# The last 64 inner columns of a gated FFN: gate and up in one product, high and low parts in one k tile

## The chip, the cores and the metric

The kernel runs on one core of one Trainium2 chip. The metric is the device time of one execution in microseconds. The time before the change is the median of three runs, 2739.53 us (2738.53 to 2741.1). Every time below of a single instruction comes from one profiled execution, which took 2738.45 us; its span, from the first to the last instruction, is 2736.7 us.

## The reference, cut to what matters

Three layers work on 512 tokens of width 1024. Each has an FFN, a mixer and a second FFN, so six FFNs in all. The first four have an inner width of 2816, which is 22 tiles of 128. The two of the last block have an inner width of 2752, which is 21.5 tiles:

```python
D_FF_2 = 2752
def swiglu_2(h, w_gate, w_up, w_down):
    return (jax.nn.silu(h @ w_gate) * (h @ w_up)) @ w_down

x = x + 0.5 * swiglu_2(rms_norm_2(x, ffn1_norm), ffn1_w_gate, ffn1_w_up, ffn1_w_down)
...
x = x + 0.5 * swiglu_2(rms_norm_2(x, ffn2_norm), ffn2_w_gate, ffn2_w_up, ffn2_w_down)
```

## The kernel before

**Layout.** Activations are kept feature-major: a tile holds 128 features in its partitions and 512 tokens in its columns. X is 8 such tiles, the inner activation of an FFN is 22 of them. A product takes a 128x128 block of weights as the stationary operand and a tile of activations as the moving one, and adds into one of 8 PSUM banks.

**Precision.** Each factor is split in a high part (float32r) and a low part (the rest), and a product is three matmuls: low weights by high activations, high by low, high by high. That is the helper `mm3` (lines 418, 419, 420). Where the profile names L418, L419 and L420 it means these three. Xh and Xl are the parts of the FFN's input, Hh and Hl those of its inner activation, wh and wl those of a chunk of weights.

**Weights.** `weight_stream` lists all weights once, as chunks of up to 128 x 1024 numbers, in the order in which TensorE takes them. Each chunk goes through a ring of three buffers (`N_RAW`): SP's `fetch` loads it to `raw` (lines 2039 to 2048) once the chunk three before it has been split; ScalarE's `high` writes wh (L889) and VectorE's `low` writes wl (L1265), both only after TensorE has finished with the chunk three before. Each of these two engines calls `use`, which splits up to two chunks ahead (`AHEAD`) of what TensorE is due to take; so the splits stand between the engine's other work, in an order fixed by the program.

**An FFN** is a stage `s`; s = 7 and s = 9 have the inner width 2752. In `ffn(s)` TensorE goes over blocks j of 256 inner columns: gate for two tiles, then up for the same two, each from two chunks of 4 k tiles by 256 columns. Block j uses banks 0 to 3 if j is even, 4 to 7 if odd; in each half the gates stand in the lower two and the ups in the upper two. For each inner tile VectorE and ScalarE then do in turn: gate times the norm factor r (VectorE, L1274), silu (ScalarE, L957), up times r, times silu (VectorE, L1274), copy to Hh (ScalarE, L920), subtract to Hl (VectorE, L1274). The down product (`residual`) makes output tiles in groups of two, two, two, one and one (`DOWN`), each over all 22 k tiles; at k tile k it waits for Hh and Hl of tile k. In s = 9 the eighth output tile is made in two halves of 256 tokens (`last_tile`).

**The odd width.** `tile_width` gives the last two inner tiles, 20 and 21, 96 columns each, 192 together. So the last block (j = 10) makes two gate and two up products that give 96 partitions each, from chunks 4 x 192 = 768 wide, and the last two k tiles of every down product contract over 96 rows (`tail` in `proj` and `last_tile`). The rows of w_down for them are laid out by a separate DMA with 96 partitions (`parts` in `chunks`), and where they share a chunk with full tiles (output tiles 6 and 7) `high` and `low` take two instructions for that chunk.

Of the kernel before, what the change touches and what calls it, by code (L numbers as in the profile page):

```python
# [13 lines left out]
D = 1024  # L14
# [81 lines left out]

def chunks(w, k0, k1, n0, n1, per=None):

    n = n1 - n0
    per = per or min(4, CAP // n)
    got = []
    for k in range(k0, k1, per * 128):
        top = min(k1, k + per * 128)
        full, rest = divmod(top - k, 128)
        nk = full + (rest > 0)
# [15 lines left out]
def chunks_ffn(wg, wu, wd, first=False):  # L123

    f, got = wg.shape[1], []
    for n0 in range(0, f, 256):
        n1 = min(f, n0 + 256)
# [4 lines left out]
        got += chunks(wg, 0, D, n0, n1, 4) + chunks(wu, 0, D, n0, n1, 4)  # L132
    return got + chunks_down(wd, f)
# [41 lines left out]
def build(nc, a, out):  # L175
    ctx = ExitStack()
    with ctx:
# [55 lines left out]
        def parts_of(n, bufs):  # L233
            parts, width, _ = stream[n]
            return [bufs[n % N_RAW][0:rows, k0 * width:(k0 + nk) * width] for rows, k0, nk, _ in parts]
# [160 lines left out]
        def tensor_program(e, w):  # L396
# [27 lines left out]
            def proj(outs, widths, kt, hi, lo, ready, hooks, tail=128):  # L424
# [4 lines left out]
                while k < kt:  # L429
                    n, h, l, nk = chunk()  # L430
                    for kk in range(nk):
                        p, last = tail if k + kk >= kt - 2 else 128, k + kk == kt - 1
                        ready(k + kk)
                        for m, wd in enumerate(widths):
                            sl = slice(sum(widths[0:m]), sum(widths[0:m + 1]))
                            names = [outs[m][1]] if last else []
                            if kk == nk - 1 and m == len(widths) - 1:
                                names.append(("used", n))
                            mm3(into[m][0:wd, :], h[0:p, kk, sl], l[0:p, kk, sl], hi[0:p, k + kk, :],
                                lo[0:p, k + kk, :], k + kk == 0, last, *names)  # L440
# [35 lines left out]
            def residual(s, tile_bank, hi, lo, kt, ready, tail=128):  # L476
                for t0, t1, _ in DOWN if s < 9 else DOWN[0:-1]:
                    proj([(tile_bank(t), ("down", s, t)) for t in range(t0, t1)], [128] * (t1 - t0), kt, hi, lo, ready,
                         None, tail)

            def last_tile(s, hi, lo, kt, tail):
# [20 lines left out]
                for part, (q0, q1) in enumerate(HALVES):  # L502
                    name = ("down", s, 7, part)
                    bank = take(LAST[part][0], name)
                    for k in range(kt):
                        if k == len(rows):
# [3 lines left out]
                        p, last = tail if k >= kt - 2 else 128, k == kt - 1  # L510
                        mm3(bank[:, q0:q1], h[0:p, kk, :], l[0:p, kk, :], hi[0:p, k, q0:q1], lo[0:p, k, q0:q1], k == 0, last,
                            *([name] if last else []))
# [7 lines left out]
            def ffn(s):  # L520
# [3 lines left out]
                for j, n0 in enumerate(range(0, f, 256)):  # L524
                    widths = [tile_width(s, 2 * j + m) for m in range(2)]
                    for side, b in (("gate", 0), ("up", 2)):
                        outs = [(4 * (j % 2) + b + m, (side, s, 2 * j + m)) for m in range(len(widths))]
                        proj(outs, widths, KT, Xh, Xl, x_ready(s) if j == 0 else lambda k: None, hooks)
# [5 lines left out]
                residual(s, lambda t: (4 + t) % 8, *H, nt, ready, tile_width(s, nt - 1))  # L534
                if s == 9:
                    last_tile(s, *H, nt, tile_width(s, nt - 1))
# [338 lines left out]
        def scalar_program(e, w):  # L875
# [3 lines left out]
            def high():  # L879
# [8 lines left out]
                for hi, src in zip(parts_of(n, wh), parts_of(n, raw)):  # L888
                    e.activation(hi, src, ACT.Copy).then_inc(whi.up(("w", n)), 1)  # L889
# [52 lines left out]
            def ffn(s):  # L942
                f, gain = FFN[s]
                nt = -(-f // 128)
                for j in range(-(-nt // 2)):
# [5 lines left out]
                    else:  # L951
                        use(4)
# [298 lines left out]
        def vector_program(e, w):  # L1251
# [3 lines left out]
            def low():  # L1255
# [8 lines left out]
                for lo, hi, src in zip(parts_of(n, wl), parts_of(n, wh), parts_of(n, raw)):  # L1264
                    e.tensor_tensor(lo, src, hi.bitcast(F), ALU.subtract).then_inc(wlo.up(("w", n)), 1)  # L1265
# [923 lines left out]
```

## Time and profile before

| | |
|---|---|
| median of 3 runs | 2739.53 us |
| the profiled execution | 2738.45 us |
| its span | 2736.7 us |
| TensorE matmuls | 12604, busy 99% of the span |
| VectorE busy | 49% |
| ScalarE busy | 33% |
| DMA | 252.3 MB, mean 92 GB/s |
| mean granted TensorE clock | 0.998 of full |
| last gate and up block of s = 7 | starts at 2038.15 us |
| down product of s = 7 | 2060.40 us to about 2180 us |
| last gate and up block of s = 9 | starts at 2581.42 us |
| down product of s = 9 | 2603.67 us to about 2726 us |

In the profile a matmul's duration (about 0.39 us) is longer than the time from its start to the start of the next (0.22 to 0.23 us), since matmuls are pipelined. So sums of durations say nothing of the time; the distance of starts does. A line of the timeline gives start, duration, engine, line, operation, output <- inputs, shape and count. In a matmul's row `128*96` is the stationary operand, 128 rows by 96 columns, and `128x512` the moving one. Some matmul records are missing from the trace, so counts are taken from the program.

### The profile page before, as it was taken

What the parts mean: (1) busy time and instruction counts of PE and PEld (TensorE: products, weight loads), DVE (VectorE), ACT (ScalarE), POOL (GpSimd) and SP (SyncE); (2) the same over time, 40 slices, a digit from 0 to 9 for tenths busy, and PEclk for the clock granted to TensorE, in tenths of its full rate; (3) what the DMA queues carried; (4) which work ended last, traced back from release to release, by engine and by line L of the source; (5) the groups of instructions that cost most, each with busy time, mean ns of one, the idle gap of its engine ahead of it and who ended that gap; (6) DMA issues with size and microseconds to landing.
All of it is one profiled execution on the core that took longest, in us unless ns stands there. A gap on an engine that the chain in (4) does not pass through costs nothing.

```text
span 2736.7 us, 31462 instructions
## 1 busy us (share of the span) xinstructions
PE 2711.6 (99%) x12604; PEld 2257.7 (82%) x12604; DVE 1341.3 (49%) x1918; ACT 900.5 (33%) x1287; POOL 135.2 (5%) x133
## 2 busy tenths in 40 slices
PE   9999999999999999999999999999999999999998
PEld 7888878888888888888888888888888898888787
DVE  5444358764443444443655444344443478644433
ACT  4232226542222323222223232223222337432221
POOL 0000004400000000000000000000000034000000
PEclk9999999999999999999999999999999999999999
DMA  4332332023333333323333323333332321233322
GB/s 158 100 94 96 95 92 72 24 93 102 99 96 95 98 98 99 98 88 101 100 99 94 93 93 98 100 96 93 101 93 91 97 78 47 62 104 98 91 91 75
DMA packets 283121, 252.30 MB, mean 92 GB/s; under 512 B 8288, under 2 KB 280800, under 8 KB 282976
## 3 DMA queue, kind: packets, MB, share of 16 engines
q1 hardware_dynamic: 282976, 250.29, 29.8%
q8 instruction: 101, 1.65, 0.2%
q14 instruction: 44, 0.36, 0.0%
HBM read 248.16 MB, written 2.10 MB: 91 GB/s over the span
## 4 chain that ended last, share of the span: by engine, by line
PE 97%; DVE 1%; ACT 1%; issue 0%; DMA 0%; POOLq 0%; POOL 0%; DVEq 0%; SPq 0%; ACTq 0%
PE bank L418 32%; PE bank L420 32%; PE bank L419 32%; PE bank L550 1%; PE bank L460 0%; PE bank L608 0%; PE bank L609 0%; DVE a_KT L1277 0%; ACT Xh L920 0%; DVE Xl L1274 0%; DVE ft L1274 0%; DMA X<-in_xT 0%; DVE fin L1277 0%; DVE wl L1265 0%; ACT a_RB L920 0%
## 5 line engine op out<-in xcount | busy, mean ns | idle before, releaser
L1265 DVE TENSOR_TENSOR wl<-raw,wh 128x1024 fp32r<-128x1024 f32 (+3 forms) x492 | 572.6, 1177 | 924.1 <-ACT wh L889 923.5
L418 PE MATMUL bank<-Xh,wl 128*128 128x512 f32 (+1 forms) x2544 | 994.0, 391 | 7.5 <-DVE wl L1265 6.6
L420 PE MATMUL bank<-Xh,wh 128*128 128x512 f32 (+1 forms) x2544 | 991.3, 390 | 0.0
L419 PE MATMUL bank<-Xl,wh 128*128 128x512 f32 (+1 forms) x2544 | 990.9, 390 | 0.0
L889 ACT ACTIVATE wh<-raw 128x1024 fp32r<-128x1024 f32 (+3 forms) x492 | 491.7, 1014 | 952.8 <-PE bank L420 947.8
L418 PEld LDWEIGHTS bank<-Xh,wl 128*128 128x128 f32 (+1 forms) x2544 | 475.8, 187 | 111.4 <-ACT wh L889 6.1
L420 PEld LDWEIGHTS bank<-Xh,wh 128*128 128x128 f32 (+1 forms) x2544 | 475.7, 187 | 102.8
L419 PEld LDWEIGHTS bank<-Xl,wh 128*128 128x128 f32 (+1 forms) x2544 | 476.0, 187 | 100.8
L418 PE MATMUL bank<-Hh,wl 128*128 128x512 f32 (+3 forms) x1078 | 415.1, 385 | 0.0
L419 PE MATMUL bank<-Hl,wh 128*128 128x512 f32 (+3 forms) x1078 | 414.9, 385 | 0.0
L420 PE MATMUL bank<-Hh,wh 128*128 128x512 f32 (+3 forms) x1078 | 414.7, 385 | 0.0
L1274 DVE TENSOR_TENSOR ft<-bank,rb 128x512 f32<-128x512 f32 (+1 forms) x264 | 181.5, 688 | 171.5 <-PE bank L420 112.2
L418 PEld LDWEIGHTS bank<-Hh,wl 128*128 128x128 f32 (+1 forms) x1078 | 202.5, 188 | 40.5
L419 PEld LDWEIGHTS bank<-Hl,wh 128*128 128x128 f32 (+1 forms) x1078 | 202.6, 188 | 40.5
L420 PEld LDWEIGHTS bank<-Hh,wh 128*128 128x128 f32 (+1 forms) x1078 | 202.5, 188 | 40.4
L920 ACT ACTIVATE Hh<-ft 128x512 fp32r<-128x512 f32 (+1 forms) x132 | 83.5, 632 | 269.0 <-DVE ft L1274 269.0
L957 ACT ACTIVATE ft<-ft 128x512 f32<-128x512 f32 (+1 forms) x132 | 83.5, 632 | 208.6 <-DVE ft L1274 208.6
L1274 DVE TENSOR_TENSOR Hl<-ft,Hh 128x512 fp32r<-128x512 f32 (+1 forms) x132 | 91.3, 692 | 92.2 <-ACT Hh L920 92.2
L1274 DVE TENSOR_TENSOR ft<-ft,ft 128x512 f32<-128x512 f32 (+1 forms) x132 | 91.4, 692 | 4.5
L917 ACT ACTIVATE Xh<-X,par 128x512 fp32r<-128x512 f32 x64 | 46.1, 723 | 128.0 <-DVE X L1277 108.4
L1895 POOL TENSOR_TENSOR r<-small,half 128x4 f32<-128x4 f32 (+1 forms) x11 | 10.5, 957 | 1376.1 <-DVE small L1283 1376.1
L1277 DVE SCALAR_TENSOR_TENSOR Xl<-X,par,Xh 128x512 fp32r<-128x512 f32 x64 | 47.8, 750 | 38.3 <-ACT Xh L917 38.0
(289 smaller groups left out, 1568.3 us busy)
## 6 DMA issues: line engine op xcount, KB each, us to landing
raw<-in_ffn_w_up SPq DMA_DIRECT2D x128, 512.0 KB, 3.9
raw<-in_ffn_w_gate SPq DMA_DIRECT2D x127, 512.0 KB, 3.6
raw<-in_ffn_w_down SPq DMA_DIRECT2D x114, 512.0 KB, 3.5
raw<-in_c_w_in SPq DMA_DIRECT2D x24, 512.0 KB, 3.6
raw<-in_w_in SPq DMA_DIRECT2D x10, 512.0 KB, 3.7
raw<-in_ffn_w_down SPq DMA_DIRECT2D x16, 256.0 KB, 2.7
raw<-in_a_w_in SPq DMA_DIRECT2D x8, 512.0 KB, 3.8
raw<-in_a_w_out SPq DMA_DIRECT2D x8, 512.0 KB, 3.4
```

What stands on the lines that cost most here:

```text
L418: e.matmul(o, ll, rh, start=start, stop=False)
L419: e.matmul(o, lh, rl, start=False, stop=False)
L420: i = e.matmul(o, lh, rh, start=False, stop=stop)
L550: e.transpose(bank[0:rows, t * 128:(t + 1) * 128], src, ident).then_inc(mm.up(name), 1)
L889: e.activation(hi, src, ACT.Copy).then_inc(whi.up(("w", n)), 1)
L917: e.activation(Xh[:, t, :], X[:, t, :], ACT.Copy, scale=col(gain, t)).then_inc(act.up(("xh", s, t)), 1)
L920: e.activation(dst, src, ACT.Copy, scale=scale).then_inc(act.up(*names), 1)
L957: e.activation(B[0:wd, :], A[0:wd, :], ACT.Silu).then_inc(act.up(("silu", s, ht)), 1)
L1265: e.tensor_tensor(lo, src, hi.bitcast(F), ALU.subtract).then_inc(wlo.up(("w", n)), 1)
L1274: e.tensor_tensor(dst, a, b, op).then_inc(dve.up(*names), 1)
L1277: e.scalar_tensor_tensor(dst, a, scalar, b, op0, op1).then_inc(dve.up(*names), 1)
L1895: e.tensor_tensor(dst, a, b, op).then_inc(pool.up(*names), 1)
```

## The change

The inner columns are cut otherwise: tiles 0 to 20 have 128 columns, and tile 21 has 64. Tile 20 gets a gate product and an up product of its own, each from one chunk of 8 k tiles by 128 columns. For tile 21 one chunk holds the 64 gate columns and the 64 up columns beside each other, and one product makes both: gate in partitions 0 to 63 of bank 1, up in partitions 64 to 127. VectorE reads up, the norm factor for it, and writes the low part of the result, in partitions 64 to 127; gate, silu and the high part stay in partitions 0 to 63. So k tile 21 of `Hh` holds the high part above and the low part below. The chunk of w_down for this k tile has its 64 rows twice, once for each half. The down product then takes two matmuls for this tile (`mm2`: low weights by both, high weights by both) and contracts over 128 rows. In the ring of chunks, the last block has three chunks and not four.

```diff
+def rows_of(w, k0, k1, n0, n1):
+    return w[k0:k1, n0:n1].rearrange("(k p) n -> p k n", p=min(128, k1 - k0))
 # chunks()
+        cut = k + full * 128
+        moves = [(0, (0, n), 0, rows_of(w, k, cut, n0, n1))] if full else []
         if rest:
-            full -= 1
-        parts = []
-        if full:
-            parts.append((128, 0, full, w[k:k + full * 128, n0:n1].rearrange("(k p) n -> p k n", p=128)))
-        if rest:
-            parts.append((64 + rest // 2, full, 2, w[k + full * 128:top, n0:n1].rearrange("(k p) n -> p k n", k=2)))
-        got.append((parts, n, nk))
+            moves += [(row, (0, n), full, rows_of(w, cut, top, n0, n1)) for row in (0, 64)]
+        got.append((moves, n, full + (rest > 0)))
 # chunks_ffn()
+    if f % 256:
+        n0, n1 = f - 192, f - 64
+        got += chunks(wg, 0, D, n0, n1, 8) + chunks(wu, 0, D, n0, n1, 8)
+        got.append(([(0, (0, 64), 0, rows_of(wg, 0, D, n1, f)), (0, (64, 128), 0, rows_of(wu, 0, D, n1, f))], 128, KT))
 # tile_width()
-            f = FFN[s][0]
-            return 64 + f % 128 // 2 if f % 128 and ht >= f // 128 - 1 else 128
+            return min(128, FFN[s][0] - 128 * ht)
 # tensor_program
+            def mm2(o, h, l, both, *names):
+                e.matmul(o, l, both, start=False, stop=False)
+                i = e.matmul(o, h, both, start=False, stop=True)
 # proj()
-                        p, last = tail if k + kk >= kt - 2 else 128, k + kk == kt - 1
+                        last = k + kk == kt - 1
...
+                            if half and last:
+                                mm2(into[m][0:wd, :], h[:, kk, sl], l[:, kk, sl], hi[:, k + kk, :], *names)
 # ffn() on TensorE
+                if f % 256:
+                    for b, name in ((0, ("gate", s, nt - 2)), (2, ("up", s, nt - 2)), (1, ("gate", s, nt - 1))):
+                        proj([(b, name)], [128], KT, Xh, Xl, lambda k: None, hooks)
+                    mm.also(("up", s, nt - 1))
 # ScalarE high(), VectorE low(): one instruction for every chunk
-                for hi, src in zip(parts_of(n, wh), parts_of(n, raw)):
-                    e.activation(hi, src, ACT.Copy).then_inc(whi.up(("w", n)), 1)
+                e.activation(part_of(n, wh), part_of(n, raw), ACT.Copy).then_inc(whi.up(("w", n)), 1)
 # ffn() on ScalarE and VectorE, last block
-                        use(4)
+                        use(4 if 2 * j < f // 128 - 1 or f % 256 == 0 else 3)
 # ffn() on VectorE
+                        low = H[1][:, ht, :]
...
+                            tt(A, gate, r, ALU.mult, ("g", s, ht))
+                            up, r, low = banks[1][64:128, :], rb[s % 2][64:128, :], H[0][64:128, ht, :]
...
-                        tt(H[1][0:wd, ht, :], A, H[0][0:wd, ht, :].bitcast(F), ALU.subtract, ("hl", s, ht))
+                        tt(low, A, H[0][0:wd, ht, :].bitcast(F), ALU.subtract, ("hl", s, ht))
 # fetch() on SP
-                for (_, _, _, src), dst in zip(parts, parts_of(n, raw)):
-                    e.dma_start(dst.rearrange("p (k n) -> p k n", n=width), src).then_inc(raw_in[r].sem, 16)
+                for row, (c0, c1), k0, src in moves:
+                    dst = raw[r][row:row + src.shape[0], 0:nk * width].rearrange("p (k n) -> p k n", n=width)
+                    e.dma_start(dst[:, k0:k0 + src.shape[1], c0:c1], src).then_inc(raw_in[r].sem, 16)
```

## Rows read from the trace of the kernel before

**Rows 1.** The page's first part: busy time of each engine and instructions.
```profile
PE 2711.6 (99%) x12604; PEld 2257.7 (82%) x12604; DVE 1341.3 (49%) x1918; ACT 900.5 (33%) x1287; POOL 135.2 (5%) x133
```

**Rows 2.** The page's fourth part: the chain that ended last, by engine.
```profile
PE 97%; DVE 1%; ACT 1%; issue 0%; DMA 0%; POOLq 0%; POOL 0%; DVEq 0%; SPq 0%; ACTq 0%
```

**Rows 3.** Groups by shape: operation, shapes, count, busy us, mean ns, idle before, releaser.
```profile
L418 PE MATMUL bank<-Xh,wl 128*128 128x512 f32 x2472 | 965.7, 391 | 7.5 <-DVE wl L1265 6.6 <-ACT g_P L973 0.8
```

**Rows 4.** Timeline, TensorE: eight k tiles into one bank, in the convolution mixer.
```profile
1310.45 0.39 PE L418 MATMUL bank<-Xh,wl 128*128 128x512 f32 x1
...
1315.89 0.39 PE L418 MATMUL bank<-Xh,wl 128*128 128x512 f32 x1
```

**Rows 5.** Timeline, TensorE, s = 7: last gate and up block, first k tiles of down.
```profile
2038.15 0.39 PE L418 MATMUL bank<-Xh,wl 128*96 128x512 f32 x1
...
2060.40 0.40 PE L418 MATMUL bank<-Hh,wl 128*128 128x512 f32 x1
...
2087.61 0.40 PE L418 MATMUL bank<-Hh,wl 96*128 96x512 f32 x1
...
2090.36 0.40 PE L418 MATMUL bank<-Hh,wl 128*128 128x512 f32 x1
```

**Rows 6.** Timeline, TensorE, s = 9: start and end of the last block.
```profile
2581.42 0.39 PE L418 MATMUL bank<-Xh,wl 128*96 128x512 f32 x1
...
2603.67 0.40 PE L418 MATMUL bank<-Hh,wl 128*128 128x512 f32 x1
```

**Rows 7.** Timeline, TensorE: k tiles 20 and 21 of single and half output tiles.
```profile
2163.93 0.40 PE L418 MATMUL bank<-Hh,wl 96*128 96x512 f32 x1
...
2165.32 0.40 PE L418 MATMUL bank<-Hh,wl 128*128 128x512 f32 x1
...
2715.79 0.28 PE L418 MATMUL bank<-Hh,wl 96*128 96x256 f32 x1
...
2716.51 0.28 PE L418 MATMUL bank<-Hh,wl 128*128 128x256 f32 x1
```

**Rows 8.** Timeline, VectorE, s = 7: around the start of the last block and its end.
```profile
2033.84 0.96 DVE L1265 TENSOR_TENSOR wl<-raw,wh 128x768 fp32r<-128x768 f32 x1 [4.48 <-ACT wh L889]
...
2040.39 0.69 DVE L1274 TENSOR_TENSOR ft<-bank,rb 128x512 f32<-128x512 f32 x1
...
2043.96 0.69 DVE L1274 TENSOR_TENSOR Hl<-ft,Hh 128x512 fp32r<-128x512 f32 x1 [0.70 <-ACT Hh L920]
2044.69 1.83 DVE L1265 TENSOR_TENSOR wl<-raw,wh 128x768 fp32r<-128x768 f32 x2
...
2066.18 0.69 DVE L1274 TENSOR_TENSOR Hl<-ft,Hh 96x512 fp32r<-96x512 f32 x1 [0.70 <-ACT Hh L920]
2067.13 2.36 DVE L1265 TENSOR_TENSOR wl<-raw,wh 128x1024 fp32r<-128x1024 f32 x2 [0.26 <-ACT wh L889]
```

**Rows 9.** Timeline, ScalarE, the same stretch; one split of a full chunk.
```profile
2043.83 1.57 ACT L889 ACTIVATE wh<-raw 128x768 fp32r<-128x768 f32 x2
2049.53 1.06 ACT L889 ACTIVATE wh<-raw 128x1024 fp32r<-128x1024 f32 x1 [4.14 <-PE bank L420]
```

**Rows 10.** Groups by shape, VectorE on 64 partitions.
```profile
L1274 DVE TENSOR_TENSOR Xl<-bank,Xh 64x512 fp32r<-64x512 f32 x16 | 11.0, 687 | 12.2 <-ACT Xh L920 11.9
```

**Rows 11.** DMA issues: count, KB each, median us from issue to landing.
```profile
raw<-in_c_w_in SPq DMA_DIRECT2D x24, 512.0 KB, 3.6
raw<-in_ffn_w_gate SPq DMA_DIRECT2D x4, 384.0 KB, 3.3
raw<-in_ffn_w_down SPq DMA_DIRECT2D x6, 192.0 KB, 2.4
```

**Rows 12.** Timeline, SP's queue: the issue of the third chunk of the last block.
```profile
2025.58 4.23 SPq L2046 DMA_DIRECT2D raw<-in_ffn_w_up  x2
```

**Rows 13.** Stretches of 2 us in the first mixer: busy times, then PEclk.
```profile
468.00:470.00 2.00, 0.17 (x2) 0.00 (x0) 1.97 (x9) 1.18 (x4) 1.43 (x2) 1.00 0.14 18
470.00:472.00 2.00, 1.88 (x12) 1.68 (x13) 1.97 (x10) 0.64 (x4) 2.00 (x7) 0.85 0.71 244
472.00:474.00 2.00, 2.00 (x10) 1.91 (x9) 1.96 (x9) 0.45 (x2) 2.00 (x3) 0.50 0.00 0
474.00:476.00 2.00, 2.00 (x13) 1.87 (x12) 0.95 (x6) 1.30 (x6) 1.39 (x4) 0.80 0.00 0
```

More of the change, by code:

```diff
@@ L125, in chunks_ffn @@
     f, got = wg.shape[1], []
-    for n0 in range(0, f, 256):
-        n1 = min(f, n0 + 256)
+    for n0 in range(0, f // 256 * 256, 256):
+        n1 = n0 + 256
         if first and n0 == 0:
@@ L231, in build, with part_of @@
         stream = weight_stream(a)
-        def parts_of(n, bufs):
-            parts, width, _ = stream[n]
-            return [bufs[n % N_RAW][0:rows, k0 * width:(k0 + nk) * width] for rows, k0, nk, _ in parts]
+        def part_of(n, bufs):
+            _, width, nk = stream[n]
+            return bufs[n % N_RAW][:, 0:nk * width]
         def views(n):
@@ L422, in mm3, with proj @@
                     i.then_inc(mm.up(*names), 1)
-            def proj(outs, widths, kt, hi, lo, ready, hooks, tail=128):
+            def mm2(o, h, l, both, *names):
+                e.matmul(o, l, both, start=False, stop=False)
+                i = e.matmul(o, h, both, start=False, stop=True)
+                if names:
+                    i.then_inc(mm.up(*names), 1)
+            def proj(outs, widths, kt, hi, lo, ready, hooks, half=False):
                 into = [take(*o) for o in outs]
@@ L438, in proj @@
                                 names.append(("used", n))
[L439 to L440 removed]
+                            if half and last:
+                                mm2(into[m][0:wd, :], h[:, kk, sl], l[:, kk, sl], hi[:, k + kk, :], *names)
+                            else:
+                                mm3(into[m][0:wd, :], h[:, kk, sl], l[:, kk, sl], hi[:, k + kk, :], lo[:, k + kk, :],
+                                    k + kk == 0, last, *names)
                     k += nk
@@ L474, in stats, with residual, last_tile @@
                 return sums, spread
-            def residual(s, tile_bank, hi, lo, kt, ready, tail=128):
+            def residual(s, tile_bank, hi, lo, kt, ready, half=False):
                 for t0, t1, _ in DOWN if s < 9 else DOWN[0:-1]:
                     proj([(tile_bank(t), ("down", s, t)) for t in range(t0, t1)], [128] * (t1 - t0), kt, hi, lo, ready,
-                         None, tail)
-            def last_tile(s, hi, lo, kt, tail):
+                         None, half)
+            def last_tile(s, hi, lo, kt):
                 rows = []
@@ L509, in last_tile @@
                         h, l, kk = rows[k]
-                        p, last = tail if k >= kt - 2 else 128, k == kt - 1
-                        mm3(bank[:, q0:q1], h[0:p, kk, :], l[0:p, kk, :], hi[0:p, k, q0:q1], lo[0:p, k, q0:q1], k == 0, last,
-                            *([name] if last else []))
+                        if k == kt - 1:
+                            mm2(bank[:, q0:q1], h[:, kk, :], l[:, kk, :], hi[:, k, q0:q1], name)
+                        else:
+                            mm3(bank[:, q0:q1], h[:, kk, :], l[:, kk, :], hi[:, k, q0:q1], lo[:, k, q0:q1], k == 0, False)
                         if part == 1 and k == 6:
@@ L1356, in ffn @@
                     else:
-                        use(4)
+                        use(4 if 2 * j < f // 128 - 1 or f % 256 == 0 else 3)
                     for ht in range(2 * j, min(2 * j + 2, nt)):
```

25 lines of the change are left out of this document (13 added, 12 removed).

## Prediction

> **What bounds the kernel now.** I read the busy times first, then the chain that ended last, then the groups by shape, and only then the timeline of the two stages that the change touches. TensorE is busy 99% of the span [rows 1] and holds 97% of the chain [rows 2]. The largest of its groups, 2472 matmuls, stood idle for 7.5 us in all, and 6.6 of those were waits for VectorE's weights [rows 3]. So the time is TensorE's, and an instruction taken from it gives back its pitch (the distance from one matmul's start to the next), as long as the weights and the inner activation still come in time. The price is the pitch and not the duration: eight k tiles of three matmuls into one bank take 5.44 us, 0.2267 us for each [rows 4], while each lasts 0.39 us.
>
> **The gate and up side.** Before, the last block of s = 7 is 2 gates and 2 ups over 8 k tiles, 2 x 2 x 8 x 3 = 96 matmuls with 96 columns of weights. They take 2060.40 - 2038.15 = 22.25 us, 0.2318 us each [rows 5]; s = 9 takes the same 22.25 us [rows 6]. After, it is three products of 8 k tiles, 72 matmuls with 128 columns. A bank that takes all eight k tiles in a row has a row of its own, at 0.2267 us [rows 4], so 72 of them are 16.32 us. Saved: 5.93 us in each FFN, 11.86 us. Of these 24 x 0.2267 = 5.44 us per FFN are the matmuls that go, and 0.49 us is the slower pitch of the narrow ones.
>
> **A rule of the notes.** The narrow block's pitch is 0.2318 us, the full one's 0.2267 [rows 4, 5]. The Trainium skill ("TensorE: Matmul & The Clock Gate", Back-to-back issue gap) gives an isolated matmul of 512 columns 518 cycles of the fast clock, whatever the number of weight columns; that would be an estimated 0.216 us for either. The trace differs in both. By that page the sum would be 64 matmuls' worth of 0.216, some 13.8 us.
>
> **The down side.** Before, the last two k tiles are six matmuls per output tile with 96 rows. After, they are five with 128 rows. For a pair of output tiles the twelve took 2090.36 - 2087.61 = 2.75 us [rows 5], and ten take 10 x 0.2267 = 2.27 us: 0.48 us saved, three pairs in each FFN, 1.44 us. For a single output tile six took 1.39 us [rows 7], and five take 1.13 us: 0.26 us saved, twice in s = 7 and once in s = 9. The halves of the last tile of s = 9 took 0.72 us for six, 0.12 us each [rows 7]; one less in each half saves 0.24 us. Down side: 1.44 + 0.52 = 1.96 us in s = 7 and 1.44 + 0.26 + 0.24 = 1.94 us in s = 9, 3.90 us.
>
> **The sum** is 11.86 + 3.90 = 15.8 us. The profiled execution (2738.45 us, span 2736.7) would come to 2722.7 us with a span of 2720.9; the median of the runs shown lies 1.1 us higher, and from it the forecast is 2739.53 - 15.8 = 2723.8 us.
>
> **What has to stay hidden: the splits.** Call T = 2038.15 the start of the last block. The third chunk is needed at T + 10.88 (two chunks of 24 matmuls). VectorE ends the two inner tiles of the block before at 2044.65, T + 6.5 [rows 8]. ScalarE starts the high part of the third chunk at 2043.83, T + 5.7, and a full chunk takes it 1.06 us [rows 9]; VectorE's low part follows at T + 6.75 and lasts 1.2 us (two took 2.36 [rows 8]), so it is ready at T + 8.0. The slack is 2.9 us. Before, the third chunk was ready at about T + 7.5 and needed at T + 11.1, 3.6 us. Two earlier splits grow from 768 to 1024 columns, 0.96 to 1.2 us on VectorE; the first steps of the tile behind them (gate, silu) shift by some 0.3 us, and then the chain waits for its up product, which ends near T anyway.
>
> The block now ends at T + 16.3 = E. In front of it VectorE's order is: low part of the third chunk, of the first down chunk (T + 8.0 to 9.2), of the second, which waits until TensorE is done with the up chunk at T + 10.88 (high, then low, to T + 13.2); then tile 20, then tile 21. Queued behind that wait is tile 20, whose gate was ready at T + 5.44; nobody needs it early. A tile's chain lasts from 2040.39 to 2044.65, 4.3 us [rows 8]: tile 20 is done at T + 17.5 = E + 1.2, tile 21 at E + 5.4. Before, both were done at 2066.87, which is 6.5 us after the block's end [rows 5, 8]. Next are the splits of the third and fourth down chunk. They follow by 0.3 to 1.5 us, the first ready at E + 7.0; TensorE needs it at E + 10.88, 3.9 us of slack against 3.0 before (ready at 2067.13 + 1.18 = 2068.3, needed at 2060.40 + 10.88 = 2071.3 [rows 5, 8]). The down product itself meets k tile 20 only 120 matmuls later, at E + 27.2, and tile 21 six later. All waits inside the change are covered, and the one behind the block is covered better. The fewer split instructions on ScalarE and VectorE (one instead of two for the last chunks of output tiles 6 and 7, one chunk less) are off the path and cost or give nothing.
>
> **Other parts.** The partition shift: two VectorE operations on tile 21 (up times r, and the low part) read and write at different partitions. No row of before shows a shifted operation. The nearest is 64 partitions from PSUM at 0.687 us [rows 10], and the full width costs 0.69 too [rows 8]; a shift could cost nothing, or, as an upper bound, one more pass of the same length, 0.69 us each. I take 0; at the bound 1.4 us more go into a slack of 3.9. A gain is excluded, since the chain isn't on the path. Banks: the last block takes banks 0, 2 and 1, read long before; down's first pair takes banks 4 and 5, whose last reading (the gate of tile 19, 2040.39 to 2041.08 [rows 8]) lies 13 us before E. Loads: 64 rows of w_down go twice, by three DMAs instead of one or two. A tail chunk of 192 KB lands in 2.4 us [rows 11]; three issues on SP, each of the size of one now, bound it at three times that, 7.2 us, and below at 2.4. It is the last chunk of six, fetched three chunks ahead of its use (at least two full chunks of TensorE, 10.9 us), so either end costs nothing. The `use(3)` keeps both splitting engines in step with three chunks.
>
> **The load of the combined chunk.** It is two DMAs of 256 KB, in pieces of 64 columns, 256 bytes; the chunk of before it had pieces of 768 bytes and landed in 3.3 us [rows 11]. The convolution's chunks are 512 KB in 1024 pieces of 512 bytes and land in 3.6 us [rows 11]. The new one has 2048 pieces: 3.6 us if bytes count, 7.2 us if pieces do. It is issued once the chunk three before it is split, at 2025.58 [rows 12], and ScalarE wants it at 2043.83 [rows 9]: 18.2 us. Both ends fit, I take zero. The Trainium skill ("DMA: Bandwidth & Descriptors", Specifications) says that a transfer wants at least 512 bytes per piece for line rate and that a smaller one is a read-modify-write. No row of before shows pieces of 256 bytes; what that rule could do here is the second rival.
>
> **The rivals.**
> *A, VectorE is late behind the shifted operations.* If the two of them cost so much that the third down chunk comes late, each microsecond above 3.9 us is TensorE's. Against it: [rows 10]. A stall has a price of its own: after a stop of 2 us in the first mixer [rows 13] the granted clock was 0.50 for some 3.4 us (0.85, 0.50 and 0.80 over three stretches of 2 us), from 1.00, that is 1.2 GHz instead of 2.4, which gives back 1.7 us less work. With a stall of 2 us in each FFN, and 1.7 us behind each, this case gives 2723.8 + 7.4 = 2731.2 us.
> *B, the combined chunk lands too late (the other side).* Its small pieces may be so slow that ScalarE waits for the load. TensorE begins to lose when landing takes more than 18.2 + 2.9 = 21.1 us, about three times the upper bound of 7.2. A stall then costs its length plus 1.7 us of clock [rows 13], in two FFNs; the whole gain of 15.8 us is lost at a stall of 6.2 us each, landing in 27.3 us, and 0.2% more than that at 30. With pieces four times as dear as in the convolution's chunk (28.8 us) the stall is 7.7 us, 2 x 9.4 = 18.8 us against 15.8: 2742.5 us, about as before, and above 30 us slower. For it: nothing in the rows but their silence.
> *C, only the count helps.* The slow pitch of 0.2318 belongs to the place and not to the 96 columns: then 72 x 0.2318 = 16.7 us and 10 and 5 matmuls at 0.229 on the down side, a loss of 0.37 and about 0.08 us per FFN: 2724.7 us. Against it: the 120 matmuls right behind the block, with the same engines beside them, take 27.21 us, 0.2268 each [rows 5].
> *D, the change doesn't do what it says:* the three products would not follow each other without a gap, because each is a new bank and a new chunk every 24 matmuls. Against it: the convolution does the same for 24 products with no gap in the one that is shown [rows 4]. I give it no time of its own; a few tenths at each of three starts lie inside the range.
>
> **How the numbers follow.** About 0.2% (5.5 us) is what a measurement of this kernel can tell from no change, so faster means below 2734.1 us. Forecast 0.84, C 0.06, A 0.06 (2731, still faster, but its longer stalls reach the middle), B 0.04, half of it at no change and half slower. Range: below, the sum against the lowest of the runs before gives 2722.7, and one more microsecond is the spread of medians, so 2721; above, C at 2724.7, the highest of the runs before less the sum (2725.3) and stalls of A's kind up to 1.5 us per FFN give 2729. Faster 0.94, within 0.2% 0.04, slower 0.02.
>
> **What would show it.** In the trace after: 72 matmuls of 128 x 128 between the last block's start and the first down matmul, 16.3 us, in both FFNs; no matmul with 96 rows or columns on Xh or Hh with 512 tokens; k tiles 20 and 21 of a pair in 2.27 us; the two FFNs 7.9 us shorter each and all else alike; idle before L418 still about 7.5 us. Rival A would show as idle time of TensorE some 11 us after the down product starts, released by wl; B as a wait of ScalarE's split for a DMA from w_gate or w_up; C as a pitch above 0.227 in the last block. The prediction is wrong if a new stretch with a granted clock of 0.5 appears in s = 7 or s = 9.

## The result and the profile after

The changed kernel takes 2723.57 us (median of four runs, 2723.0 to 2724.64) against 2740.32 us (four runs, 2738.53 to 2742.66): a ratio of 0.9940, 95% interval 0.9928 to 0.9952, 16.75 us less. A second set of five runs gave 2723.57 us again, ratio 0.9939 (0.9926 to 0.9953). The forecast was 2723.8 us.

The profiled execution took 2723.5 us, its span is 2721.7 us; the span of before was 2736.7, so it shows 15.0 us. The page's first and fourth part after:

```profile
PE 2696.8 (99%) x12539; PEld 2252.2 (83%) x12539; DVE 1341.3 (49%) x1912; ACT 899.7 (33%) x1281; POOL 135.1 (5%) x133
PE 97%; DVE 1%; ACT 1%; issue 0%; DMA 0%; POOLq 0%; POOL 0%; DVEq 0%; SPq 0%; ACTq 0%
```

There are 65 matmuls fewer, as the edit says: 24 in each last block, 8 in the down product of s = 7, 7 and two halves in that of s = 9. The busy shares, which answer to [rows 1], and the chain [rows 2] have not moved, so this page alone would not tell where the 15 us went. The largest group, by shape as in [rows 3], comes with the line numbers of the new file (L423, L424 and L425 are `mm3`, L431 and L432 `mm2`, L1282 the low split, L1292 VectorE's tensor_tensor, L907 the high split, L2070 the load):

```profile
L423 PE MATMUL bank<-Xh,wl 128*128 128x512 f32 x2520 | 984.8, 391 | 7.5 <-DVE wl L1282 6.6 <-ACT g_P L991 0.8
```

Idle before it is 7.5 us as before. No new wait has come, and from 480 us to 2714 us, which takes in both FFNs, the mean granted clock is 1.00: the stretch at 0.5 that would have made the prediction wrong is in neither. The timeline of TensorE in s = 7 answers to [rows 5], with one line of s = 9 and two of its last halves:

```profile
2039.33 0.39 PE L423 MATMUL bank<-Xh,wl 128*128 128x512 f32 x1
...
2055.65 0.39 PE L423 MATMUL bank<-Hh,wl 128*128 128x512 f32 x1
...
2084.21 0.39 PE L431 MATMUL bank<-Hh,wl 128*128 128x512 f32 x1
2084.44 0.39 PE L432 MATMUL bank<-Hh,wh 128*128 128x512 f32 x1
2084.67 0.39 PE L431 MATMUL bank<-Hh,wl 128*128 128x512 f32 x1
2084.89 0.39 PE L432 MATMUL bank<-Hh,wh 128*128 128x512 f32 x1
2085.12 0.39 PE L423 MATMUL bank<-Hh,wl 128*128 128x512 f32 x1
...
2590.89 0.39 PE L423 MATMUL bank<-Hh,wl 128*128 128x512 f32 x1
```

The last block lasts 2055.65 - 2039.33 = 16.32 us, to the hundredth what the sum had. A pair of output tiles lasts 2085.12 - 2055.65 = 29.47 us, where [rows 5] had 2090.36 - 2060.40 = 29.96. The splits behind the block, which answer to [rows 8]:

```profile
2046.10 2.36 DVE L1282 TENSOR_TENSOR wl<-raw,wh 128x1024 fp32r<-128x1024 f32 x2 [0.26 <-ACT wh L907]
...
2058.19 0.69 DVE L1292 TENSOR_TENSOR ft<-bank,rb 64x512 f32<-64x512 f32 x1 [0.70 <-ACT ft L975]
2058.92 0.68 DVE L1292 TENSOR_TENSOR ft<-ft,ft 64x512 f32<-64x512 f32 x1
2060.30 0.69 DVE L1292 TENSOR_TENSOR Hh<-ft,Hh 64x512 fp32r<-64x512 f32 x1 [0.70 <-ACT Hh L938]
2061.25 2.42 DVE L1282 TENSOR_TENSOR wl<-raw,wh 128x1024 fp32r<-128x1024 f32 x2 [0.27 <-ACT wh L907]
```

The first and the third of the 64-partition lines are the shifted operations: 0.69 us each, no dearer than an unshifted one. With T the start of the last block and E its end, as in the prediction, the third chunk of the block is ready at 2046.10 + 1.18 = 2047.28, T + 7.95; tile 21 ends at 2060.99, E + 5.3; the third down chunk is ready at 2062.46, E + 6.8. The combined chunk's two loads were issued at 2026.77 and 2027.19, and each took a few microseconds:

```profile
2026.77 0.37 SPq L2070 DMA_DIRECT2D raw<-in_ffn_w_gate  x1
2027.19 0.57 SPq L2070 DMA_DIRECT2D raw<-in_ffn_w_up  x1
...
raw<-in_ffn_w_up SPq DMA_DIRECT2D x2, 256.0 KB, 4.7
```

**Stage by stage.** I take the distance between the small matmuls that sum squares, of which one group of eight stands near the start of each stage, and the first down matmul within an FFN; the last row ends at the first of two matmuls of the final norm, just behind the last down product. In microseconds, from the profiled executions:

| stretch | before | after | difference |
|---|---|---|---|
| through s = 2 (the first mixer), from its statistics to those of s = 3 | 137.70 | 139.00 | +1.30 |
| s = 3 to s = 6, up to the statistics of s = 7 | 1256.83 | 1256.83 | 0.00 |
| s = 7 to its first down matmul | 230.38 | 224.44 | -5.94 |
| s = 7, from there to the statistics of s = 8 | 131.45 | 129.38 | -2.07 |
| s = 8 | 181.44 | 181.42 | -0.02 |
| s = 9 to its first down matmul | 230.38 | 224.44 | -5.94 |
| s = 9, from there to the last matmuls | 125.90 | 123.75 | -2.15 |

The two FFNs give back 8.01 and 8.09 us, 16.1 in all; the medians differ by 16.75, and their interval (13.2 to 19.7 us) holds both. Of the last row's 2.15 us, 2.03 lie before the last down matmul and 0.12 in the norm behind it. The 1.3 us that the profiled span doesn't show were lost in a stage that the change leaves alone: there the clock stayed at half for longer (below).

### The profile page after: what moved, and what is told of

Its sections match the earlier page's. It is cut to its first block, busy times and chain, and to the rows that moved or that the text cites. A ratio compares the mean times of both kernels' runs of the same rounds, so it can differ in the third digit from the quotient of the medians.

```text
span 2721.7 us, 31322 instructions
## 1 busy us (share of the span) xinstructions
PE 2696.8 (99%) x12539; PEld 2252.2 (83%) x12539; DVE 1341.3 (49%) x1912; ACT 899.7 (33%) x1281; POOL 135.1 (5%) x133
## 4 chain that ended last, share of the span: by engine, by line
PE 97%; DVE 1%; ACT 1%; issue 0%; DMA 0%; POOLq 0%; POOL 0%; DVEq 0%; SPq 0%; ACTq 0%
PE bank L423 32%; PE bank L425 32%; PE bank L424 32%; PE bank L569 1%; PE bank L475 0%; PE bank L627 0%; PE bank L628 0%; DVE a_KT L1295 0%; ACT Xh L938 0%; PE bank L431 0%; PE bank L432 0%; DVE Xl L1292 0%; DVE ft L1292 0%; DMA X<-in_xT 0%; DVE fin L1295 0%
## 5 line engine op out<-in xcount | busy, mean ns | idle before, releaser
L1282 DVE TENSOR_TENSOR wl<-raw,wh 128x1024 fp32r<-128x1024 f32 (+2 forms) x486 | 572.2, 1190 | 912.1 <-ACT wh L907 911.4
L423 PE MATMUL bank<-Xh,wl 128*128 128x512 f32 x2528 | 987.9, 391 | 7.5 <-DVE wl L1282 6.6
L425 PE MATMUL bank<-Xh,wh 128*128 128x512 f32 x2528 | 985.1, 390 | 0.0
L424 PE MATMUL bank<-Xl,wh 128*128 128x512 f32 x2528 | 985.1, 390 | 0.0
L907 ACT ACTIVATE wh<-raw 128x1024 fp32r<-128x1024 f32 (+2 forms) x486 | 490.9, 1024 | 940.9 <-PE bank L425 936.1
L423 PEld LDWEIGHTS bank<-Xh,wl 128*128 128x128 f32 x2528 | 474.8, 188 | 108.2 <-ACT wh L907 6.1
L425 PEld LDWEIGHTS bank<-Xh,wh 128*128 128x128 f32 x2528 | 474.8, 188 | 100.3
L424 PEld LDWEIGHTS bank<-Xl,wh 128*128 128x128 f32 x2528 | 474.9, 188 | 98.3
L423 PE MATMUL bank<-Hh,wl 128*128 128x512 f32 (+1 forms) x1061 | 408.5, 385 | 0.0
L425 PE MATMUL bank<-Hh,wh 128*128 128x512 f32 (+1 forms) x1061 | 408.3, 385 | 0.0
L424 PE MATMUL bank<-Hl,wh 128*128 128x512 f32 (+1 forms) x1061 | 408.3, 385 | 0.0
L1292 DVE TENSOR_TENSOR ft<-bank,rb 128x512 f32<-128x512 f32 x264 | 181.7, 688 | 167.9 <-PE bank L425 107.4
L424 PEld LDWEIGHTS bank<-Hl,wh 128*128 128x128 f32 x1061 | 199.3, 188 | 39.9
L425 PEld LDWEIGHTS bank<-Hh,wh 128*128 128x128 f32 x1061 | 199.3, 188 | 39.7
L423 PEld LDWEIGHTS bank<-Hh,wl 128*128 128x128 f32 x1061 | 199.3, 188 | 39.6
L1292 DVE TENSOR_TENSOR Hl<-ft,Hh 128x512 fp32r<-128x512 f32 x130 | 90.0, 692 | 90.8 <-ACT Hh L938 90.8
L1292 DVE TENSOR_TENSOR ft<-ft,ft 128x512 f32<-128x512 f32 x132 | 91.4, 692 | 4.5
```

The source lines that it names most:

```text
L423: e.matmul(o, ll, rh, start=start, stop=False)
L424: e.matmul(o, lh, rl, start=False, stop=False)
L425: i = e.matmul(o, lh, rh, start=False, stop=stop)
L907: e.activation(part_of(n, wh), part_of(n, raw), ACT.Copy).then_inc(whi.up(("w", n)), 1)
L1282: e.tensor_tensor(part_of(n, wl), part_of(n, raw), part_of(n, wh).bitcast(F), ALU.subtract).then_inc(wlo.up(("w", n)), 1)
L1292: e.tensor_tensor(dst, a, b, op).then_inc(dve.up(*names), 1)
```

## The experiments

The theory: the gain is the number of matmuls taken off TensorE times their pitch, plus the slower pitch of the 96-column ones, and all else has cover. Seven kernels were run for the terms and the covers, and four more for what these left open. Their edits are cut to what matters; `...` stands for lines left out.

**The changed kernel again**, beside the three below.

> The changed kernel once more, beside the three below. My theory (count of matmuls times pitch, and the narrow pitch and its switches gone) gives 16.0 us less than before: 8.0 in each of the two FFNs. If the step from 15.8 forecast to the measured medians were more than noise, the saving would come out near 16.8 again; if the missing 1.2 us of the profiled span is the clock after the stall in the first mixer, that stretch and no other shows it again or not, by chance.

It took 2723.57 us (2721.38 to 2724.7) beside a before of 2740.34 (22 runs). In its profile the FFNs are those of the table to 0.01 us. Only the first mixer differs again, 140.66 us. So the medians gave 16.8 us once more, where the stages of both profiles give 16.1: what the other 0.7 us are, no stage shows, and the intervals are wide enough for them to be noise.

**Only the gate and up side** (the same edit stands in `last_tile`).

```diff
-                                mm2(into[m][0:wd, :], h[:, kk, sl], l[:, kk, sl], hi[:, k + kk, :], *names)
+                                mm3(into[m][0:wd, :], h[0:64, kk, sl], l[0:64, kk, sl], hi[0:64, k + kk, :],
+                                    lo[0:64, k + kk, :], False, True, *names)
...
-                        low = H[1][:, ht, :]
+                        low = H[1][0:wd, ht, :]
...
-                            up, r, low = banks[1][64:128, :], rb[s % 2][64:128, :], H[0][64:128, ht, :]
+                            up, r = banks[1][64:128, :], rb[s % 2][64:128, :]
```

> Only the gate and up side of the change: three products of 24 in the last block, but the low part of tile 21 stands in its own buffer and k tile 21 of the down product is three matmuls over 64 rows, as three-part products are. By my sum 15 matmuls of 0.2267 us and two halves of 0.12 us come back, 3.6 us, and some 0.1 to 0.4 us more for switching between 128 and 64 rows: 3.6 to 4.0 us slower than the changed kernel, about 12.2 us faster than before. If the down side were worth nothing (hidden by something else), it would be as fast as the changed kernel.

It took 2732.20 us (ratio to before 0.9970, 0.9959 to 0.9982), 8.6 us slower than the changed kernel and not 3.6 to 4.0. The trace puts all of it in the two down products: 133.38 and 127.83 us, 4.00 and 4.08 more than in the changed kernel. That is even 1.9 us each more than before. Where it goes, from TensorE's timeline of s = 7 around the first visit to k tile 21:

```profile
2083.61 0.39 PE L425 MATMUL bank<-Hh,wh 128*128 128x512 f32 x1
2083.93 0.49 PE L423 MATMUL bank<-Hh,wl 64*128 64x512 f32 x1
2084.26 0.39 PE L424 MATMUL bank<-Hl,wh 64*128 64x512 f32 x1
...
2085.19 0.39 PE L425 MATMUL bank<-Hh,wh 64*128 64x512 f32 x1
2085.51 0.50 PE L423 MATMUL bank<-Hh,wl 128*128 128x512 f32 x1
2085.84 0.40 PE L424 MATMUL bank<-Hl,wh 128*128 128x512 f32 x1
```

The starts are 0.32 and 0.33 us apart where the stationary operand goes from 128 to 64 rows, and again where it goes back, instead of 0.23. So both sides of my theory were tried at once, count and switches; the run with a third matmul, below, parts them.

**Only the down side.** Tiles of 128 and 64 columns, gate and up in 96 matmuls as before, `mm2` in the down product. The edit is against the changed kernel; VectorE then reads up from partitions 0 to 63, and only the low part is shifted.

```diff
-        got += chunks(wg, 0, D, n0, n1, 8) + chunks(wu, 0, D, n0, n1, 8)
-        got.append(([(0, (0, 64), 0, rows_of(wg, 0, D, n1, f)), (0, (64, 128), 0, rows_of(wu, 0, D, n1, f))], 128, KT))
+        got += chunks(wg, 0, D, f - 192, f, 4) + chunks(wu, 0, D, f - 192, f, 4)
...
-                    for b, name in ((0, ("gate", s, nt - 2)), (2, ("up", s, nt - 2)), (1, ("gate", s, nt - 1))):
-                        proj([(b, name)], [128], KT, Xh, Xl, lambda k: None, hooks)
+                    for side, b in (("gate", 0), ("up", 2)):
+                        proj([(b, (side, s, nt - 2)), (b + 1, (side, s, nt - 1))], [128, 64], KT, Xh, Xl,
+                             lambda k: None, hooks)
```

> Only the down side: tiles of 128 and 64 columns, gate and up made by 96 matmuls (half of them 64 columns wide), the low part of tile 21 in the lower half of the high part's k tile, two matmuls for it. By my sum 3.9 us faster than before from the down side, and 0.1 to 0.5 us per FFN from the pitch of the block if the 64-column matmuls are slow (0.2318) or not: 4.2 to 5.2 us faster than before. If the whole gain were the block's, it would be no faster than before.

It took 2734.42 us (ratio 0.9981, 0.9972 to 0.9990), 5.9 us faster than before by the medians (the interval allows 2.7 to 7.7), 4.7 by the stages of its trace: 2.05 and 2.13 us in the down products (129.40 and 123.77, the changed kernel's own) and 0.28 in each block. By the stages it lies in the 4.2 to 5.2 us that were expected, by the medians above them. The down side's worth is as forecast, and it doesn't need the other side.

**The block with 128 weight columns**, in the kernel before.

```diff
+                            at = n % N_RAW
+                            if wd == 96:
+                                c = kk * 192 + 96 * m
+                                mm3(into[m][:, :], wh[at][:, c:c + 128], wl[at][:, c:c + 128], hi[:, k + kk, :],
+                                    lo[:, k + kk, :], k + kk == 0, last, *names)
+                                continue
```

> The kernel before, with 128 weight columns in each of the 96 matmuls of the last block instead of 96 (the 32 columns more are read from what stands behind in the buffer, and the 32 rows that they fill in the bank are read by nobody). My theory: the pitch goes from 0.2318 to 0.2267 us, the block from 22.25 to 21.76 us in both FFNs, 1.0 us in all. Rival C, the slow pitch belongs to the place: the block stays at 22.25 us and the time is that of before.

It took 2738.70 us (ratio 0.9996, 0.9987 to 1.0005). The block's first matmul and the first of the down product, in s = 7:

```profile
2036.99 0.39 PE L418 MATMUL bank<-Xh,wl 128*128 128x512 f32 x1
...
2059.24 0.39 PE L418 MATMUL bank<-Hh,wl 128*128 128x512 f32 x1
```

22.25 us, as with 96 columns. The narrow stationary operand is not what makes the block slow, or not alone. Nor is it the place (rival C): the changed kernel runs at 0.2267 us there. A full block of 128 columns makes its products in pairs too, like the narrow one, and has 0.227 us, so the order of the banks isn't it either. What is left is how the weights lie: 192 columns, 768 bytes, from one k tile to the next, and the second inner tile at byte 384. Two kernels take these apart.

**Another layout for the same 96 matmuls.**

```diff
+        if n1 - n0 == 192:
+            for w in (wg, wu):
+                for k in (0, 512):
+                    rows = w[k:k + 512, n0:n1].rearrange("(k p) n -> p k n", p=128)
+                    got.append(([(128, 0, 4, rows)], 256, 4))
+            continue
...
+                            if wd == 96:
+                                sl = slice(SECOND * m, SECOND * m + 96)
```

(In the kernel before, with the load as two DMAs, the second to column `SECOND`, 128 in the first kernel and 96 in the second.)

> The kernel before, with the same 96 matmuls of 96 columns in the last block, but the chunk laid out with 256 columns for each k tile and the two inner tiles at columns 0 and 128 of them (byte offsets 0 and 512), by two DMAs per chunk. Neither the number of weight columns nor the place in the program changes. The 128-column run at the old layout kept the slow block (22.25 us), so my term 'narrow columns are slow' has fallen. Theory now: the layout of the weights (a distance of 768 bytes between k tiles, an offset of 384) is slow; then this block takes 21.76 us in both FFNs, 1.0 us less in all. Rival: 96 columns or any layout but the changed kernel's own are slow, 22.25 us.

> The same, 256 columns for each k tile, but the second inner tile at column 96 (byte offset 384). If the distance of 768 bytes is what is slow, the block takes 21.76 us as above. If the offset of 384 bytes is, the second tile's half of the matmuls stay slow: between 21.9 and 22.25 us.

Both took the time of before: 2740.51 us (ratio 1.0, 0.9991 to 1.0009) and 2739.13 us (the same ratio and interval). The blocks in s = 7, first the one with the tiles at columns 0 and 128, then at 0 and 96:

```profile
2039.24 0.39 PE L425 MATMUL bank<-Xh,wl 128*96 128x512 f32 x1
...
2061.32 0.39 PE L425 MATMUL bank<-Hh,wl 128*128 128x512 f32 x1
```

```profile
2038.84 0.39 PE L425 MATMUL bank<-Xh,wl 128*96 128x512 f32 x1
...
2061.09 0.40 PE L425 MATMUL bank<-Hh,wl 128*128 128x512 f32 x1
```

22.08 us and 22.25 us: a pitch of 0.2300 and 0.2318. Neither reaches 21.76, so this theory in its plain form has fallen too. The distance of 768 bytes isn't needed for the slow pitch, as 1024 with an offset of 384 is as slow. With narrow operands the offset of 384 costs 0.17 us of the 0.49, and the other 0.32 stay when both tiles start at multiples of 512 bytes; a full operand in the old layout costs all 0.49. The two don't add up, and what they have in common stays open. Each is worth under 1 us in all. (In the run of the down side alone the block, with tiles of 128 and 64 columns, the second at byte 512 and the k tiles 768 bytes apart, took 21.97 us, 0.2289 for each.)

**A third matmul over full rows.** The changed kernel with one more product of the low weights in `mm2`; the output holds that small term twice.

```diff
                 e.matmul(o, l, both, start=False, stop=False)
+                e.matmul(o, l, both, start=False, stop=False)
```

> The changed kernel with three matmuls for k tile 21 of the down product instead of two, all over 128 rows: the product of the low weights is done twice, so the output has that small term once too often. The run with three matmuls over 64 rows lost 8.1 us in the two down products, where my sum had 3.6. Theory: 3.6 us are the 15 matmuls and two halves, and the other 4.5 us are the change between 128 and 64 rows, so this run is 3.6 us slower than the changed kernel (1.8 in each down product). Rival: a third matmul costs 8.1 us by itself.

It took 2727.27 us (ratio 0.9954, 0.9941 to 0.9966), 3.7 us more than the changed kernel. The down products lasted 131.19 and 125.52 us, 1.81 and 1.77 more, 3.58 in all. So the 15 matmuls and two halves cost 3.6 us as the sum had it, and the other 4.5 us of the run with three matmuls over 64 rows are the switches between 128 and 64 rows. There are 11 visits to k tile 21, since a pair of output tiles makes its six matmuls in one: five in s = 7, four and two halves in s = 9. That is 0.41 us a visit on average; the four slow starts shown above, 0.32 and 0.33 us each way, make 0.39 of it for a pair.

**VectorE made late.** The low part of tile 21 is written again and again, with the same result.

```diff
+                        for _ in range(4 if wd == 64 else 0):
+                            tt(low, A, H[0][0:wd, ht, :].bitcast(F), ALU.subtract)
+                            w.wait_ge(dve, HERE)
                         tt(low, A, H[0][0:wd, ht, :].bitcast(F), ALU.subtract, ("hl", s, ht))
```

(10 in place of 4 in the second.)

> The changed kernel with the shifted low part of tile 21 done five times instead of once (same result), each 0.73 us with its wait: VectorE is 2.9 us later with the split of the third down chunk. The trace of the changed kernel has it ready at 2062.45 and needed at 2055.65 + 10.88 = 2066.5, 4.1 us of slack. Theory: 2.9 is hidden, the time is that of the changed kernel. If the slack were none, 2.9 us per FFN, 5.8 us slower.

> The same, eleven times: 7.3 us later, 3.2 us more than the slack of 4.1. Theory: TensorE stands idle 3.2 us at the third down chunk of both FFNs, and loses up to 1.7 us more each if the granted clock falls to half behind it as it did behind the 2 us stop in the first mixer: 6.4 to 9.8 us slower than the changed kernel. If the ends of the down product aren't TensorE's but another's, nothing.

With four: 2723.35 us (ratio 0.9940, 0.9924 to 0.9957), nothing. With ten: 2734.66 us (ratio 0.9978, 0.9969 to 0.9987), 11.1 us more than the changed kernel. VectorE, then TensorE in s = 7 and s = 9:

```profile
2060.34 7.89 DVE L1292 TENSOR_TENSOR Hh<-ft,Hh 64x512 fp32r<-64x512 f32 x11 [0.70 <-ACT Hh L938]
2068.25 3.50 DVE L1282 TENSOR_TENSOR wl<-raw,wh 128x1024 fp32r<-128x1024 f32 x3
...
2069.58 0.77 PE L423 MATMUL bank<-Hh,wl 128*128 128x512 f32 x1 [2.86 <-issue]
...
2610.87 0.47 PE L423 MATMUL bank<-Hh,wl 128*128 128x512 f32 x1 [2.85 <-issue]
```

TensorE was idle for 2.9 us at the third down chunk, and the start of its next matmul was 3.0 us late (3.25 us behind the one before it, 2066.33 in s = 7, in place of 0.23), where 7.3 less 4.1 us of slack had said 3.2. The down products lasted 133.84 and 128.47 us, 4.46 and 4.72 more: 1.4 and 1.7 us above the stop itself. The granted clock says why, in stretches of 2 us behind the stop (the number before the last two is PEclk):

```profile
2069.00:2071.00 2.00, 1.42 (x4) 1.16 (x5) 2.00 (x3) 0.00 (x0) 0.00 (x0) 0.51 0.07 24
2071.00:2073.00 2.00, 2.00 (x7) 1.63 (x6) 0.75 (x1) 0.00 (x0) 0.00 (x0) 0.64 0.56 138
2073.00:2075.00 2.00, 2.00 (x10) 1.62 (x10) 0.00 (x0) 0.00 (x0) 0.00 (x0) 1.00 1.01 354
```

1.2 GHz and then 2.4 again, 3.4 us at the half clock; the price of rival A, a stop and its clock, is as it was put. The time is above the 6.4 to 9.8 us that were expected. The 9.2 us of the two products lie inside; 1.6 us more came in the mixer of s = 8 (183.02 us against 181.42), 10.8 in all in the profile. That mixer isn't touched by the edit. It has a stop of 1.3 us in every profile, and here the granted clock fell to half for 3.4 us behind it; in three other profiles of kernels whose edits don't touch it the same happened (183.0, 183.0 and 182.9 us), in the other nine it did not.

**The combined chunk made slow to load**, in pieces of 8 columns (W = 8) and of 2 (W = 2).

```diff
-        got.append(([(0, (0, 64), 0, rows_of(wg, 0, D, n1, f)), (0, (64, 128), 0, rows_of(wu, 0, D, n1, f))], 128, KT))
+        got.append(([(0, (o + c, o + c + W), 0, rows_of(w, 0, D, n1 + c, n1 + c + W))
+                     for o, w in ((0, wg), (64, wu)) for c in range(0, 64, W)], 128, KT))
```

> The changed kernel with the combined chunk loaded by 16 DMAs in pieces of 8 columns, 32 bytes: 16384 pieces instead of 2048. Rival B's threshold is a landing 21.1 us after the first issue. The 16 issues alone take about 6.7 us at 0.42 us each; by the chunk of 2048 pieces, whose two halves landed 4.2 and 4.7 us after their issue, eight times the pieces would be at most some 38 us. If the landing stays under 21 us the time is that of the changed kernel; if it takes L, each of the two FFNs loses L - 21.1 us and up to 1.7 us for the clock. Theory: pieces are cheap, under 21 us, no change. Rival B: a wait of the high split for a DMA and idle TensorE at the third product.

> The combined chunk by 64 DMAs in pieces of 2 columns, 8 bytes. Each issue takes SP 0.82 us in the run with 16 DMAs (6.57 us for eight), so 64 take some 52 us; the last lands about 55 us after the first issue, 34 us beyond the threshold of 21.1. Theory (rival B's mechanism at a size where it must bite): TensorE stands idle some 34 us before the third product in both FFNs, with 1.7 us of clock behind: about 70 us slower than the changed kernel. If fetches behind it in the same queue are late as well, a few us more.

With 8 columns: 2723.59 us (ratio 0.9939, 0.9924 to 0.9953), nothing. SP's queue shows why: sixteen issues take 13 us (6.7 had been expected), the pieces of one DMA land in 3 us, and the whole is there by some 16 us after the first issue, still under 21.1.

```profile
2028.11 6.57 SPq L2072 DMA_DIRECT2D raw<-in_ffn_w_gate  x8
2034.72 6.39 SPq L2072 DMA_DIRECT2D raw<-in_ffn_w_up  x8
...
raw<-in_ffn_w_gate SPq DMA_DIRECT2D x16, 32.0 KB, 3.1
```

With 2 columns: 2799.12 us (ratio 1.0221, 1.0206 to 1.0237), 75.6 us more than the changed kernel. ScalarE's split of the chunk, and TensorE's third product:

```profile
2081.99 1.06 ACT L909 ACTIVATE wh<-raw 128x1024 fp32r<-128x1024 f32 x1 [37.18 <-DMA raw<-in_ffn_w_up]
...
2084.45 0.77 PE L425 MATMUL bank<-Xh,wl 128*128 128x512 f32 x1 [34.37 <-DVE wl L1284]
```

The first issue was at 2026.47, so the load had landed after 55.5 us, and TensorE was idle for 34.37 us; by the distance of starts the next matmul was 34.5 us late. 55.5 - 34.5 = 21.0 us is the landing at which it begins to lose, against the 21.1 of the forecast. In the second FFN it was idle for 34.68 us, 34.8 by the starts. The stretches up to the down product grew by 36.62 and 37.54 us, 2.1 and 2.7 us more than the stops. That is the clock: over 2084 to 2090 us the stretches of 2 us had 0.50, 0.50 and 0.83, some 4.7 us at 1.2 GHz, of which the first 0.45 lie before TensorE started again at 2084.45; the other 4.2 are 2.1 us of work lost. The profiled execution took 2797.34 us, 1.8 below the median, and so shows 73.8 of the 75.6 us.

## Why the prediction was right

**The block, 11.86 us: right in size, wrong in one reason.** 5.94 us in each FFN was measured, 5.93 forecast. The 5.44 of these that are 24 matmuls stand. That size doesn't hang on the reason, as 22.25 us was read and 16.32 counted from rows. The 0.49 is real as well, since the new products run at 0.2267 us, but I called it the price of narrow columns, and the block with 128 columns at the old places kept all of it. It is a matter of how the weights lie and of their width together, and the changed kernel leaves both behind at once; the cause of the slow pitch stays open. Rival C, that the pitch belongs to the place, is refuted by the changed kernel's own rows; its doubt about the reason was right, its place was not.

**The rule on the isolated matmul.** The stages show 16.1 us, this kernel's own pitch had said 15.8. By the 518 cycles that the Trainium skill ("TensorE: Matmul & The Clock Gate", Back-to-back issue gap) gives for an isolated matmul the sum was an estimated 13.8; the measurement decides against it here, where no matmul is isolated and the pitch is 0.2267 us.

**The down side, 3.90 us: 4.1 measured.** From the first to the last down matmul s = 7 gave 2.06 us and s = 9 2.03; the stages of the table have 4.22 with the norm behind. I priced the six or twelve narrow matmuls by their own stretch. What the sum left out are the slower starts right behind them (before, the five behind the first pair's narrow ones were 0.228 to 0.236 us apart, and then 0.227 again); with 128 rows throughout nothing switches any more.

**The covers.** All held, and nearly to the number: third chunk ready at T + 7.95 (8.0 forecast), tile 21 at E + 5.3 (5.4), third down chunk at E + 6.8 (7.0), needed at E + 10.88. The slack of 4 us was shown from both sides, with 2.9 us of delay hidden and 7.3 paid. The shifted operations cost what unshifted ones do, 0.69 us. The extra loads of w_down's rows cost nothing: TensorE waits for none of them, and they land in 2.2 to 2.9 us (medians).

**Rival B** was possible in kind and far in size. Its threshold of 21.1 us was measured at 21.0, and its load lands some 5 us after the first issue. The Trainium skill ("DMA: Bandwidth & Descriptors", Specifications) warns of pieces under 512 bytes; the trace agrees that they are dearer, 4.7 us for 256 KB in pieces of 256 bytes against 3.6 us for 512 KB in pieces of 512 [rows 11] (two of the small ones were in flight at once, so the piece alone isn't priced), and yet it did not reach the time.

**Rival D** did not happen: the three products follow each other with no gap, all 72 starts of each block 0.226 or 0.227 us apart.

**How near the number is, is partly luck.** 2723.57 us against 2723.8 is closer than the saving itself, 16.75 us against 15.8: the forecast was taken off a median of three runs, 2739.53, and with the fourth the median of before is 2740.32.

**The missing 1.3 us of the span** are the clock's. Behind the stop of 2 us in the first mixer [rows 13] the clock stayed at half for about 3.4 us in the profile of before, and longer after the change:

```profile
470.00:472.00 2.00, 1.98 (x14) 1.80 (x14) 1.96 (x9) 0.69 (x3) 2.00 (x6) 0.94 0.67 232
472.00:474.00 2.00, 2.00 (x12) 2.00 (x11) 1.93 (x10) 0.35 (x2) 2.00 (x3) 0.50 0.00 0
474.00:476.00 2.00, 2.00 (x9) 1.81 (x9) 1.34 (x9) 1.80 (x6) 1.66 (x5) 0.50 0.00 0
476.00:478.00 2.00, 2.00 (x7) 1.47 (x6) 1.26 (x5) 1.22 (x3) 2.00 (x2) 0.50 0.00 0
478.00:480.00 2.00, 2.00 (x18) 1.98 (x16) 1.09 (x4) 1.07 (x3) 1.60 (x1) 0.86 0.17 40
```

The granted clocks of the five stretches are short of full by 0.06, 0.5, 0.5, 0.5 and 0.14, 1.7 in sum; times 2 us, and doubled since the short clock is the half one, that is 6.8 us at 1.2 GHz. It differs from one execution to the next: the second profile of the same kernel had 0.50 over five such stretches (140.66 us for the mixer), and the variant of before with 128 columns had 1.00 in all of them (136.21 us). Over all profiles this stage took 136.2, 137.7, 139.0 or about 140.6 us, in steps of about 1.5 us; none of the kernels changes anything in it. That the change has no part in it isn't shown by so few: the four profiles of before and its variants have 136.2, 137.7, 139.0 and 139.0, the nine of the changed kernel and its variants 139.0 seven times, 140.7 and 140.6. A loss of this kind isn't seen in the medians, which differ by more than the two FFNs gave.

## What to carry to other kernels

Where TensorE is the bound throughout, a tile that is cut ragged costs as much as a full one (here 0.2318 us a matmul with 96 columns, 0.2267 with 128), and two half tiles that share the moving operand, or the stationary one, are worth one product; priced by the distance of starts, not by durations, the saving came out within 2% here (15.8 us for 16.1). Give each neighbour a deadline (when is the chunk needed, when is it ready) and the covers can be forecast too. And it pays to keep the row count of the stationary operand the same throughout: three matmuls over 64 rows made the down product of s = 7 2.19 us longer than three over 128.

## What the runs showed of the hardware that I had not expected

- A switch of the stationary operand from 128 to 64 rows and back costs 0.41 us per visit here, nearly two matmuls. With the last two k tiles as three matmuls over 128 rows and three over 64, the down product of s = 7 took 133.38 us, with six over 96 rows 131.45.
- 96 weight columns with the two tiles at bytes 0 and 512 have a pitch of 0.2300 us, at 0 and 384 0.2318; 128 columns at the old places (k tiles 768 bytes apart, the second inner tile at 384) 0.2318, and 128 at multiples of 512 bytes 0.2267. Why stays open.
- Two VectorE operations of 64 partitions with input and output 64 partitions apart take 0.69 us, as without the shift.
- After the same stop of 2 us the granted clock was at half for 0, 3.4, 6.8 or about 10 us from one profile to another, and behind the stop of 1.3 us in the mixer of s = 8 for 0 (nine profiles) or 3.4 us (four). The first moves this kernel by up to 4.4 us, a quarter of what the change gives, and the second by 1.6, so the stages of a trace tell more here than the difference of two spans.
